# Selecting the rows of experts 0 and 1 before the ranking of the experts in a decoder-layer kernel

## What is computed

```
def _post_block(x, feats, w_o, ln1_g, ln1_b, moe, ln2_g, ln2_b):
    h = _layer_norm(DEEPNORM_ALPHA * x + feats @ w_o, ln1_g, ln1_b)
    return _layer_norm(DEEPNORM_ALPHA * h + _hmoe(h, *moe), ln2_g, ln2_b)

# in _hmoe: 4 groups of 8 experts, 2 experts of one group for each token
    grp = jnp.argmax(g_logit, -1)
    p_top, i_top = lax.top_k(jax.nn.softmax(e_logit, -1), EXPERT_TOPK)
    gate = p_grp * p_top / p_top.sum(-1, keepdims=True)
    eid = (grp[:, None] * EXPERTS_PER_GROUP + i_top).reshape(-1)
    ...
    def expert_block(args):                 # a block of rows of one expert e
        xb, e = args
        hb = jax.nn.silu(xb @ w_gate[e]) * (xb @ w_up[e])
        return hb @ w_down[e]
```

## Time and profile before

| | us |
|---|---|
| median of three runs | 1797.9 |
| the three runs | 1792.35 to 1799.26 |
| profiled execution | 1795.99 |
| its span (first to last instruction) | 1794.2 |
| TensorE busy | 1495.8 (83%) |
| VectorE busy | 577.9 (32%) |
| mean share of TensorE's full clock granted | 0.904 |
| moved by DMA | 597.41 MB |

### The profile page before, as it was taken

The page is one execution under the profiler, slowest core; times in us unless marked ns, Lnnn a source line. Parts: engine busy times, 40 slices in busy tenths (PEclk is TensorE's granted clock), DMA queues, the critical chain, the costliest instruction groups (busy, mean ns, idle before and its releaser), DMA issues.

```text
span 1794.2 us, 25175 instructions
## 1 busy us (share of the span) xinstructions
PE 1495.8 (83%) x10680; PEld 870.2 (49%) x10680; DVE 577.9 (32%) x1210; ACT 269.8 (15%) x618; POOL 70.9 (4%) x88
## 2 busy tenths in 40 slices
PE   3999999999698999948997867878769677888684
PEld 2787788888576577723333322323223223232231
DVE  0744476687454111163321211112102111121026
ACT  0012311201263100021111100110101011111110
POOL 2110000111110000000000000000000000000000
PEclk9999999999898899969998988889889888788895
DMA  9996387896899898319989999999999999999991
GB/s 279 315 294 202 103 264 239 254 315 196 312 365 379 290 293 313 138 37 418 418 331 419 419 419 419 419 419 419 419 419 418 419 419 420 419 420 419 419 387 53
DMA packets 236255, 597.41 MB, mean 333 GB/s; under 512 B 13984, under 2 KB 173280, under 8 KB 179808
## 3 DMA queue, kind: packets, MB, share of 16 engines
q1 hardware_dynamic: 216320, 499.22, 73.6%
q0 software_dynamic: 9792, 75.57, 10.8%
q10 hardware_dynamic: 10024, 20.94, 3.2%
HBM read 586.63 MB, written 17.48 MB: 337 GB/s over the span
## 4 chain that ended last, share of the span: by engine, by line
DMA 33%; PE 26%; SPq 2%; DVE 2%; ACT 1%; issue 1%; ACTq 0%; DVEq 0%
DMA arena<-in_w_up 32%; PE ps L1816 7%; PE ps L1871 6%; PE ps L1901 5%; PE ps L1845 4%; PE ps L1892 2%; SPq L1394 2%; DMA arena<-in_w_down 2%; PE ps L1852 0%; PE ps L1807 0%; ACT arena L1461 0%; DVE arena L1773 0%; DVE arena L1774 0%; SPq L1396 0%; PE ps L1805 0%
## 5 line engine op out<-in xcount | busy, mean ns | idle before, releaser
L1871 PE MATMUL ps<-arena 128*32 128x256 f32 x4352 | 318.8, 439 | 178.4 <-DMA arena<-in_w_up 176.9
L638 PE MATMUL ps<-arena 128*128 128x264 f32 x1664 | 382.9, 388 | 28.4 <-DMA arena<-in_w_in 28.4
L638 PEld LDWEIGHTS ps<-arena 128*128 128x128 f32 x1664 | 313.2, 191 | 82.1 <-issue 27.0
L1871 PEld LDWEIGHTS ps<-arena 128*32 128x32 f32 x4352 | 170.5, 122 | 326.5 <-issue 272.6
L1845 PE MATMUL ps<-arena 128*32 128x512 f32 (+1 forms) x816 | 188.1, 1030 | 10.7 <-DVE arena L1664 10.7
L1679 DVE TENSOR_TENSOR arena<-arena,ps 64x256 f32<-64x256 f32 x34 | 14.4, 425 | 546.6 <-ACT arena L1465 546.6
L1892 PE MATMUL ps<-arena 128*32 128x512 f32 x1088 | 160.6, 693 | 3.1 <-DMA arena<-in_w_down 3.1
L1816 PE MATMUL ps<-arena 128*128 128x264 f32 x512 | 122.0, 396 | 1.4 <-PEq L2007 1.4
L1478 ACT COPY arena<-ps 32x512 f32<-32x512 f32 x136 | 78.4, 576 | 254.1 <-PE ps L1892 252.9
L1901 PE MATMUL ps<-arena,keep 128*128 128x512 f32 (+3 forms) x216 | 113.3, 685 | 3.5 <-issue 3.5
L1816 PEld LDWEIGHTS ps<-arena 128*128 128x128 f32 x512 | 97.6, 194 | 24.1 <-issue 7.8
(11 more groups left out here) (404 smaller groups left out, 1012.0 us busy)
## 6 DMA issues: line engine op xcount, KB each, us to landing
arena<-in_w_gate SPq DMA_DIRECT2D x128, 1024.0 KB, 26.6
arena<-in_w_up SPq DMA_DIRECT2D x128, 1024.0 KB, 27.0
arena<-in_w_down SPq DMA_DIRECT2D x128, 1024.0 KB, 27.1
arena<-in_w_in SPq DMA_DIRECT2D x52, 1024.0 KB, 7.1
arena<-in_w_o SPq DMA_DIRECT2D x16, 1024.0 KB, 11.0
arena<-in_w_cmp_k POOLq DMA_DIRECT2D x8, 512.0 KB, 8.1
arena<-in_w_cmp_v POOLq DMA_DIRECT2D x8, 512.0 KB, 6.8
arena<-in_win_k SPq DMA_DIRECT2D x8, 512.0 KB, 7.1
```

Source lines behind the costliest of these rows:

```text
L638: last = pe.matmul(ps[:, n % 2, 0:T], ring[:, n % FRONT_SLOTS, k, :], x[:, k, :], start=(k == 0), stop=(k == KT - 1))
L1871: last = pe.matmul(ps[BS * q:BS * q + BS, 0, 0:CHUNK // 2], xs[:, kk * 4 + i, :], ring[:, s, at:at + CHUNK // 2], start=(k == 0), stop=(k ...
```

## The change

The slots of experts 0 and 1 need no ranking: their blocks are fixed, and the place in the block is `before`. The change computes the expert number of each row (`eid`) before the wait for the counts, and from it a `code` that is valid for experts 0 and 1 and far off (`-FAR`) for the others. Right behind `c_cum` it adds the rank and selects only the 64 slots of blocks 0 and 1. The ranking and the full `code` follow unchanged, then `turned(0)` and the order of the experts, and then a second selection of the other 64 slots, those of blocks 2 and 3. So `d_sel` counts one more from there on, and TensorE waits for the second selection ahead of the gather of block 2.

```diff
-    rank, ovb, more = sm(2, 3), sm(2, 3), sm(2, 3)
+    eid, rank, ovb, more = sm(2, 3), sm(2, 3), sm(2, 3), sm(2, 3)
 ...
             v.tensor_tensor(gate_w[:, 1], m2, es, ALU.mult)
 
+            for k in (0, 1):
+                last = v.tensor_tensor(prod[:, k], flat(e12[k]), r_("experts").unsqueeze(1).broadcast_to([P, 3, NE]), ALU.mult)
+            done.link(last)
+            done.link(v.tensor_reduce(eid, prod, AX_X, ALU.add))
+            done.link(v.tensor_scalar(code, eid, float(N_FIRST), -FAR, ALU.is_ge, ALU.mult))
+            done.link(v.scalar_tensor_tensor(code, eid, float(BS), code, ALU.mult, ALU.add))
+
             v.wait_ge(S["c_cum"], 1)
             counts = ps[:, 6, 32:64]
             before = ps[:, 5, 0:96].rearrange("p (t e) -> p t e", t=3)
+            def select(of, first, at, n, over=None):
 ...
+            for k in (0, 1):
+                last = v.tensor_tensor(prod[:, k], flat(e12[k]), before, ALU.mult)
+            done.link(last)
+            done.link(v.tensor_reduce(rank, prod, AX_X, ALU.add))
+            done.link(v.tensor_tensor(code, code, rank, ALU.add))
+            done.link(v.tensor_scalar(more, rank, float(BS), -FAR, ALU.is_ge, ALU.mult))
+            done.link(v.tensor_tensor(code, code, more, ALU.add))
+            select(code, 0, 0, N_FIRST * BS)
+
             done.link(v.tensor_tensor(keys, counts, r_("counts"), ALU.mult))
 ...
-            select(code, 0, 0, P)
             turned(0)
 ...
             v.tensor_copy(m.order[0:1], order_f[0:1]).then_inc(S["c_order"], 1)
+            select(code, N_FIRST * BS, N_FIRST * BS, P - N_FIRST * BS)
 ...
                     if (b + 1) % 4 == 0:
-                        pe.wait_ge(S["d_sel"], (b + 1) // 4 + 1)
+                        pe.wait_ge(S["d_sel"], (b + 1) // 4 + 2)
+                    if b + 1 == N_FIRST:
+                        pe.wait_ge(S["d_sel"], 2)
                     gather(b + 1, BS * ((b + 1) % 4))
 ...
-                    pe.wait_ge(S["d_sel"], N_GROUP + i + 1)
+                    pe.wait_ge(S["d_sel"], N_GROUP + i + 2)
                     gather(NB + i, 64)
```

More of the change, by code:

```diff
@@ L1619, in _, with link @@
             before = ps[:, 5, 0:96].rearrange("p (t e) -> p t e", t=3)
+            def select(of, first, at, n, over=None):
+                def link(ins, name):
+                    if over is None:
+                        done.link(ins)
+                    else:
+                        ins.then_inc(S[name], 1)
+                        v.wait_ge(S[name], over + 1)
+                cols = slice(at, at + n)
+                link(v.tensor_scalar(code_g, of, float(first), None, ALU.subtract), "o_code")
+                for t, (_, rows) in enumerate(TOK):
+                    iota = r_("slots", rows)[:, 0:n]
+                    c0, c1 = code_g[0:rows, 0, t:t + 1], code_g[0:rows, 1, t:t + 1]
+                    v.tensor_scalar(pick[0:rows, t, cols], iota, c0, None, ALU.is_equal)
+                    v.tensor_scalar(pick_w[0:rows, t, cols], iota, c0, gate_w[0:rows, 0, t:t + 1], ALU.is_equal, ALU.mult)
+                    last = v.tensor_scalar(pick_1[0:rows, t, cols], iota, c1, gate_w[0:rows, 1, t:t + 1], ALU.is_equal, ALU.mult)
+                link(last, "o_eq")
+                for t, (_, rows) in enumerate(TOK):
+                    iota = r_("slots", rows)[:, 0:n]
+                    c1 = code_g[0:rows, 1, t:t + 1]
+                    v.scalar_tensor_tensor(pick[0:rows, t, cols], iota, c1, pick[0:rows, t, cols], ALU.is_equal, ALU.add)
+                    last = v.tensor_tensor(pick_w[0:rows, t, cols], pick_w[0:rows, t, cols], pick_1[0:rows, t, cols], ALU.add)
+                last.then_inc(S["d_sel"], 1)
+            for k in (0, 1):
[6 more added lines that the diff above has]
+            select(code, 0, 0, N_FIRST * BS)
             done.link(v.tensor_tensor(keys, counts, r_("counts"), ALU.mult))
@@ L1641, in _ @@
             done.link(v.tensor_tensor(code, code, more, ALU.add))
[L1643 to L1665, removed]
             per_row = [gb_x[:, j].rearrange("p (n a) -> p a n", a=4).unsqueeze(3).broadcast_to([P, 4, 4, BS]) for j in (0, 1)]
```

## The result

The changed kernel takes 1786.89 us (median of 5 runs, 1783.35 to 1789.13) and the kernel before 1794.32 us beside it (5 runs, 1792.07 to 1799.26): a ratio of 0.9947, 95% interval 0.993 to 0.9964, so it is faster. The first is the highest gain of the three, and the intervals of all three overlap. The profiled execution took 1786.89 us, span 1785.1, against 1794.2 before. Source lines from L1617 on stand further down in the changed file. `gather` is L1861 there, `turn` L1868, `hidden` L1887, `down` L1908, `combine` L1917. A count in a row is one of records: each float32 matmul of the source has two (a gather is 12 matmuls and x24), a transpose has one.

What follows compares the result with a forecast made beforehand. The prediction took the expert-weight stream as the bound, its two holes tied to the router's chain before the gather. Zero for hidden work and -6.4 us at the gather took 1796.4 to 1790.0 us, range 1785.5 to 1795.5.

Steps and rivals of the forecast that it cites:

- the sum: All steps together: 0 for the early work, -6.4 us from counts to gather, 0 for everything behind it.
- (c): First selection on 64 columns instead of 128: 1.1 us saved, 2.86 us left of 3.96; gather 6.4 us earlier in all.
- (a): Added VectorE operations ahead of the counts' wait: 1.26 us, hidden in 1.91 us of idle, cost zero.
- R1: Rival: TensorE's clock pays back more around the weight-stream holes; gain 8.2 to 11.7 us, chance 0.12.
- (b): Between counts and first selection, the 6.73 us ranking moves behind the selection; 1.46 us of short operations stays.
- (d): Ranking behind the first selection, beside the gather: 6.73 us in a 7.36 us gap, 0.63 us room, no cost.
- (e): Order of the experts right behind block 0's scaling: needed for chunk 40, 5 us of cover, nothing late.
- (f): Second selection, 2.86 us, ahead of the overflow slots: block 0's multiply 0.29 us late, absorbed by stalls for up-weights.
- R2: Rival: ranking outlasts its gap or low clock after 848 us lasts longer; 2 to 4.5 us left, chance 0.10.
- R3: Rival: low clock over block 3's whole hidden step adds 7.4 us; ends 1.0 us slower, 1797.4, chance 0.03.
- R4: Rival: second hole's end not tied to the stream's restart, so no gain, 1796.4 us, chance 0.03.

Runs made afterwards that it cites:

- The three comparisons: The unchanged changed kernel timed three times beside the kernel before: ratios 0.9947, 0.9974 and 0.9968.
- move_full: Changed kernel with the first selection over all 128 slots again, the second selection kept: ratio 0.9987 to the kernel before.
- halves_only: Kernel before with the selection cut into two halves of 64 slots, the ranking left ahead of both: ratio 0.999 to the kernel before.
- rank_delay5: Changed kernel with five linked 32 x 32 comparisons (6.3 us) between the first selection and the ranking: ratio 0.9992 to the kernel before.
- gather_delay5: Changed kernel with five linked 32 x 32 comparisons (6.3 us) ahead of the first selection: ratio 0.9994 to the kernel before.
- after_again: Changed kernel, unedited, traced a second time and timed again: ratio 0.9974 to the kernel before, median 1790.68 us.
- late_delay3: Changed kernel with three linked comparisons (3.8 us) behind the second selection: ratio 0.9965 to the kernel before.
- after_third: Changed kernel, unedited, traced and timed a third time: ratio 0.9968 to the kernel before, median 1788.24 us.
- early5_again: Second run of the changed kernel with block 5's hidden step moved ahead of combine(0): ratio 0.9954 to the kernel before, median 1787.21 us.
- warm2: Changed kernel with 16 filler matmuls ahead of each of two up-weight waits in block 2's hidden step: ratio 0.9985 to the kernel before, median 1793.16 us.
- after: First trace of the changed kernel, unedited: 1786.89 us, ratio 0.9947 to the kernel before.

## Why the prediction was right or wrong

**What was wrong** is the call "within 0.5%", with a chance of 0.82. The mechanism was right, and the time, 1786.89 us, lies in the range, 3.1 us under the forecast. Two steps failed. One is the sentence "About 0.5%, 9 us, is what a measurement of this kernel can tell from no change". Nothing that had been measured said so, and the first comparison has an interval of 0.17% to either side, 3 us, so even the forecast shift of 6.4 us is clear of no change. The other is the sum, which put everything outside the change's own place at nothing. In the first pair of traces it was not: the start of the phase gave 1.4 us and the clock in the middle 1.7. With these, the 6.4 us less 0.4 for (c) and 0.1 for (a), plus 0.1 for the rest come to the 9.1 us of the spans (the ratio says 9.5). The prediction had the clock only as a rival, R1, and no term for the start, though the last issue scatters over 9 us between traces. Its level before, 1796.4 us, was 2 us above the 1794.3 that five runs gave.

The size of the forecast is good in part by luck. The three comparisons together give 6.6 us, and the traces 6.4 from the last issue to the restart, just what was forecast. But that is 5.9 us at the gather and some 0.5 us behind it, in the transposes and the first hidden matmuls, which the prediction did not have and which the change is not shown to cause.

**(a)** Right but for a small cost. The added operations ran under the wait for the ones-matmul, of which 0.85 us is left instead of 1.91. The counts are read 16.36 to 16.38 us behind the last issue in every trace with them and 16.29 or 16.30 in the four without, so they cost 0.07 to 0.09 us and not nothing.

**(b)** Right: from the counts to the first selection 781.49 - 780.04 = 1.45 us against 1.46. The operand in PSUM added nothing that shows.

**(c)** Mis-sized. The selection took 784.76 - 781.49 = 3.27 us and not 2.86. The halving is worth 0.69 us instead of 1.1, as move_full and halves_only confirm. The step of a comparison fell from 0.20 us to 0.17 (781.70 to 781.87). The prediction compared a 32-column operation with a constant to a 128-column one with its operand in a per-partition column, and took the whole difference for columns. The rule of the Trainium skill (VectorE: DVE Perf Modes, "The perf-mode tier table (the rule you actually need)"), which was weighed and not taken, was right: by its rate and the page's clock of 0.96 GHz, 64 columns at half a cycle each are an estimated 0.033 us, and the trace has 0.03 for the comparison with one such operand and 0.04 for that with two (0.26 to 0.22). The six sums save 0.06 or 0.07 us each (0.20 to 0.14, 0.27 to 0.20). By the rule the prediction worked out a shift of 6.05 us, and from the counts to the gather it became 5.97.

**(d)** Right, 0.64 us of room against 0.63, and rank_delay5 shows what lies beyond it. One gain was not foreseen: the gather to the restart takes 11.6 to 12.3 us in the traces with the early selection against 12.35 to 12.50 in the three with the old one. The four transposes are 0.91 or 0.66 us long there and 1.11 in the old kernel. That goes with a rise of the clock during the gather (1.00 at 788 to 790 us in the changed kernel, 0.50 until 804 in the one before). halves_only (11.68, 0.66) and gather_delay5 (12.26, 0.84), whose gathers come as late as in the old kernel or nearly so, had it too, so it is no property of the early start.

**(e)** Right: chunk 40 was issued at 804.48 us, 1.7 us behind the end of the hidden step (1.4 before), and the stream had no hole there. **(f)** Right in its outcome: block 0's product started 15.45 us behind the scaling (15.18 forecast). It was not late in the first trace, where the hidden step itself was longer, and 0.86 us late in after_again; 3.0 us were absorbed in late_delay3.

**The rivals.** R1 was in part what the first trace shows, and its own sign was there: the clock was 1.00 from 842 to 846 us. It got 1.6 us of its 3.5 (it took the full-clock length of the 32 matmuls as 1.73 us, and it is 1.93). But the kernel before had a middle as short in its second trace, and after_again had none of it, so it is scatter of both. The rule of the Trainium skill on stalls (TensorE: Matmul & The Clock Gate, "HAM oscillation — how this bites in real kernels") agrees with seven of the traces, where the part behind the second stall took 3.2 to 3.6 us. It does not account for move_full, gather_delay5, after_third and early5_again, with 1.93 us behind a stall of 3.05, nor for the drop in warm2. R2 is excluded for (d). Its other half, the low clock behind 848 us, came in after_again, with 4.3 us compared with after. R3 was not seen: block 3's hidden step took 6.91 us in all chains. R4 is refuted by gather_delay5 and by the table.

Open is why the clock falls where it does, and what moves the start of the phase by up to 9 us from one execution to the next.

## What to carry to other kernels

When a weight stream stops on a full ring, look for the consumer that frees the first slot, and take off its path whatever does not decide the first block; such work can run beside the first block if it is shorter than the gap that it goes into (6.7 us in 7.4 here). Before calling a change too small to measure, look at the interval that several runs of each kernel give (0.13% to 0.21% here), not at the spread of single runs. Cut the traces at events that both kernels share and compare stretch by stretch: here the change repeats to 0.02 us, while whole runs scatter by more than 10. Closing one hole by reordering moves it to the next late release, so look at what is pushed back.

## What the runs showed of the hardware

Halving the columns of a float32 comparison with a per-partition operand from 128 to 64 saves 0.03 to 0.04 us of 0.20 to 0.26, and of a sum of two such tiles 0.06 us of 0.20. A gather takes 5.50 us with a granted clock of 0.50 and 5.42 with 1.00, both in the kernel before: it hardly depends on the clock, while the hidden and down steps do (3.57 against 1.93 us, 5.27 against 3.57).

```profile
792.00:797.00 5.00, 4.97 (x24) 0.76 (x24) 0.00 (x0) 0.00 (x0) 0.00 (x0) 0.50 0.00 0
810.00:814.00 4.00, 4.00 (x24) 0.43 (x16) 1.97 (x6) 0.00 (x0) 0.00 (x0) 1.00 1.01 424
```
```profile
809.34 5.42 PE L1845 MATMUL ps<-arena 128*32 128x512 f32 x24
```

TensorE's granted clock fell to 0.50 behind such a gather in warm2, with no wait for weights and only 0.44 us of other idle time ahead of it.
